# A two-layer decoder trunk on one Trainium2 core: first steps, up-panel products and delta-rule groups put in another order, and sums of squares on ScalarE

## The chip, the cores and the metric

The kernel runs on one core of a Trainium2 chip. The metric is the device time of one execution in microseconds. Five engines matter: PE (TensorE: matmuls and transposes; its weight loads are listed apart as PEld), DVE (VectorE), ACT (ScalarE), POOL (GpSimd), and SP, which issues the DMAs. Each engine takes its own instructions strictly in the order in which the program issues them, and they meet only through semaphores.

## The reference

The input is 256 tokens by 2048 features. Layer 0 mixes tokens with latent attention, layer 1 with a chunked gated delta rule; each also attends to 256 memory tokens, and each is followed by a squared-ReLU MLP. The parts that the change touches:

```python
mem_kv = mem @ mem_w_kv[i]
qkv = silu(causal_depthwise_conv(h[..., :3 * MIX_WIDTH], conv_w))      # 4 taps
q = l2_normalize(q); k = l2_normalize(k)    # x * rsqrt(sum(x * x, -1) + 1e-6), by head
kb = k * beta
L = where(strict, einsum(kb, k) * decay, 0)
u, w = triangular_solve(L + I, [v * beta, kb * exp(gc)])
a_qk = where(tril, einsum(q, k) * decay, 0)
# for each chunk of 64 tokens:
v_new = u - w @ state; o = q_dec @ state + a_qk @ v_new
state = state * g_last + k_dec.T @ v_new
o = rms_norm(o, o_norm) * silu(z)
x = layer_norm(ALPHA * x + y)
ff = square(relu(x @ mlp_w1[i])) @ mlp_w2[i]
```

## The kernel before, in words

**Weights.** They are read from HBM in chunks of 256 rows by 512 columns (512 KB), 8 chunks a panel. SP loads chunk c into one of four `raw` buffers once chunk c-4 has been split. ACT copies it to `whi` (L1031), rounded to fp32r; DVE takes the rest into `wlo` (L1394). Activations are split alike, and a product is whi by hi, whi by lo and wlo by hi, all on PE. `feed(n)` on ACT and on DVE stands for the next n splits in that engine's order; ACT's split of c waits until PE has used chunk c-4.

**Products.** `panel_t` puts 128 weight columns into PE and moves 256 tokens past them, three matmuls per block (L534, L536, L538). `panel_r` moves 512 weight columns (L587 to L589). `panel_up`, the first half of the MLP, moves hi and lo of the tokens in one matmul of 512 columns past whi (L561, "wide" below), and 256 columns past wlo (L563, "narrow"), in the order wide, narrow, wide, narrow: 16 matmuls a chunk, 128 chunks in all, 1024 pairs from k = 0 and 1024 from k = 1.

**First steps.** In 16 steps PE turns (transposes) two blocks of `mem`, later of `x`, and multiplies one chunk of the memory's key panel (steps 0 to 7, `panel_t`) or value panel (8 to 15, `panel_r`). Step k issues turn k+1 and then chunk k. DVE copies turn k+1 out (`first_out`, L1411), then takes the low part of turn k (`first_low`, L1427), then splits chunk k+1; ACT makes the high part between them (`first_hi`, L1052).

**Delta-rule groups.** Twelve heads run as three groups g of four. A group has panels q, k, v and z; q, k and v each go through a convolution (ACT scales one tap, L1279; DVE adds three, L1777; ACT takes tanh, L1283; DVE finishes, L1784), are turned into rows by PE (`conv_turns`, L852) and copied out by ACT (`rows_out`, L1290). DVE sums the squares of q and k rows (`row_sums`: a product L1805 and a reduction L1812 for each), POOL takes the power (L1993), DVE scales k and q (L1805). In `gdn` PE turns k, kb and q (L886, L891, L894), builds the decays (L899, L902), turns the decayed q (L908), forms the two score products (L912, L916), inverts the triangular matrix in six levels (L925 for level 0; L929, L939 and L942 for the others, with POOL masking the next level's block, L2093), and walks four chunks of the state. The 16 chunks of panel z and of the next group's q, called b0 to b15 here, are spread between these steps by `beside(g, i, n)`, so that PE has work while others answer.

The order is written out by hand for each engine; nothing is planned at run time. PSUM has two banks for turns, two `side` banks, and two pairs for panels, and `panel_free` counts emptied panels.

## Time and profile before

| | |
|---|---|
| median of 3 runs | 2517.56 us (2516.83 to 2519.83) |
| profiled execution | 2513.61 us, its span 2511.9 us |
| PE busy | 2399.0 us, 96% |
| PE weight loads | 2087.2 us, 83% |
| DVE / ACT / POOL busy | 59% / 42% / 10% |
| DMA | 417.10 MB, mean 166 GB/s |
| up-panel wide / narrow matmuls | 2048 of each, 399 / 281 ns each |

The "busy" of a matmul overlaps that of the next one: what a matmul costs is the distance between two starts, and this is what is read below. In the span, the first steps take about 0 to 75 us, layer 0's mixer and output to 360, its MLP to 1080, the three delta-rule groups 1155 to 1665, and the rest is layer 1's output and MLP. The slices in which PE is well below full are the first, those of the attention, and those of the delta-rule groups.

### The profile page before, as it was taken

How to read it: one execution, taken by the hardware profiler on the slowest of the kernel's cores; microseconds unless marked ns; L12 is line 12 of the kernel's file. 1: busy time of each engine (PE TensorE's matmuls, PEld its weight loads, DVE VectorE, ACT ScalarE, POOL GpSimd, SP SyncE). 2: the span in 40 equal slices, each digit the busy share in tenths (PEclk: the TensorE clock that was granted, in tenths of full speed). 3: DMA queues.
4: the chain of work that ended last, by engine and by line, in shares of the span. 5: the costliest groups of instructions: out<-in, count | busy, mean ns of one | idle time of the engine just before them, and what ended most of it. 6: DMA issues, size and time to landing. Idle time of an engine off the chain costs nothing.

```text
span 2511.9 us, 35407 instructions
## 1 busy us (share of the span) xinstructions
PE 2399.0 (96%) x13577; PEld 2087.2 (83%) x13577; DVE 1472.8 (59%) x1562; ACT 1058.3 (42%) x1244; POOL 240.9 (10%) x221
## 2 busy tenths in 40 slices
PE   7999989999999999999899899989899999999997
PEld 6897778888888888889799798878788888888885
DVE  4654567546555556576747648445765565555565
ACT  3455434434444444354424324233443443443443
POOL 0051001001000001000121211210010010000000
PEclk9999999999999999999999999989999999999998
DMA  5663356565566565655414325226455655666654
GB/s 203 201 169 109 114 197 193 193 193 184 193 184 193 195 190 185 209 168 168 135 51 143 93 60 165 62 75 211 128 191 201 191 186 193 181 201 193 189 192 159
DMA packets 234624, 417.10 MB, mean 166 GB/s; under 512 B 23761, under 2 KB 42474, under 8 KB 232938
## 3 DMA queue, kind: packets, MB, share of 16 engines
q1 hardware_dynamic: 233114, 410.73, 51.3%
q10 hardware_dynamic: 1360, 4.19, 0.4%
q8 instruction: 116, 1.90, 0.3%
q14 instruction: 34, 0.28, 0.0%
HBM read 412.77 MB, written 2.10 MB: 165 GB/s over the span
## 4 chain that ended last, share of the span: by engine, by line
PE 47%; issue 39%; DVE 8%; POOL 4%; ACT 1%; DMA 1%; POOLq 0%; ACTq 0%; DVEq 0%
PE quad L561 10%; PE quad L587 6%; PE quad L588 6%; PE quad L589 6%; PE quad L563 5%; PE quad L534 3%; PE quad L536 3%; PE quad L538 3%; DVE wlo L1394 2%; DVE cv L1777 2%; POOL hl L2061 1%; PE quad L929 1%; PE quad L942 1%; PE quad L939 1%; ACT whi L1031 1%
## 5 line engine op out<-in xcount | busy, mean ns | idle before, releaser
L1394 DVE TENSOR_TENSOR wlo<-raw,whi 128x1024 fp32r<-128x1024 f32 x760 | 977.3, 1295 | 720.0 <-ACT whi L1031 717.2
L1031 ACT ACTIVATE whi<-raw 128x1024 fp32r<-128x1024 f32 x760 | 798.8, 1058 | 991.4 <-PE quad L589 520.0
L561 PE MATMUL quad<-xs,whi 128*128 128x512 f32 x2048 | 724.2, 399 | 7.8 <-DVE xs L1657 3.7
L563 PE MATMUL quad<-xs,wlo 128*128 128x256 f32 x2048 | 574.7, 281 | 0.0
L587 PE MATMUL quad<-whi,hh 128*128 128x512 f32 x1344 | 529.3, 394 | 5.2 <-DVE hl L1532 3.8
L589 PE MATMUL quad<-whi,hl 128*128 128x512 f32 x1344 | 524.0, 390 | 0.0
L588 PE MATMUL quad<-wlo,hh 128*128 128x512 f32 x1344 | 523.8, 390 | 0.0
L561 PEld LDWEIGHTS quad<-xs,whi 128*128 128x128 f32 x2048 | 386.5, 189 | 103.1 <-issue 5.5
L563 PEld LDWEIGHTS quad<-xs,wlo 128*128 128x128 f32 x2048 | 388.4, 190 | 0.1
L587 PEld LDWEIGHTS quad<-whi,hh 128*128 128x128 f32 x1344 | 252.8, 188 | 60.8 <-issue 7.2
L589 PEld LDWEIGHTS quad<-whi,hl 128*128 128x128 f32 x1344 | 252.7, 188 | 53.1
L588 PEld LDWEIGHTS quad<-wlo,hh 128*128 128x128 f32 x1344 | 252.8, 188 | 51.7
L534 PE MATMUL quad<-xs,whi 128*128 128x256 f32 x704 | 204.1, 290 | 4.2 <-DVE wlo L1394 4.0
L536 PE MATMUL quad<-xs,whi 128*128 128x256 f32 x704 | 200.5, 285 | 0.0
L538 PE MATMUL quad<-xs,wlo 128*128 128x256 f32 x704 | 200.4, 285 | 0.0
L2061 POOL TENSOR_TENSOR hl<-relu,hh 128x1024 fp32r<-128x1024 f32 x32 | 81.0, 2530 | 1198.7 <-ACT hh L1214 1198.7
L534 PEld LDWEIGHTS quad<-xs,whi 128*128 128x128 f32 x704 | 136.3, 194 | 7.6 <-DVE wlo L1394 5.5
L538 PEld LDWEIGHTS quad<-xs,wlo 128*128 128x128 f32 x704 | 136.4, 194 | 0.0
L536 PEld LDWEIGHTS quad<-xs,whi 128*128 128x128 f32 x704 | 136.3, 194 | 0.0
L1686 DVE TENSOR_TENSOR relu<-quad,low 128x1024 f32<-128x1024 f32 x32 | 39.2, 1225 | 50.8 <-ACT low L1210 50.8
L2093 POOL TENSOR_TENSOR qr<-nt,level 128x512 f32<-128x512 f32 x36 | 53.3, 1495 | 156.4 <-DVE nt L1843 81.0
L587 PE MATMUL quad<-whi,xs 128*128 128x512 f32 x160 | 64.6, 404 | 0.0
(285 smaller groups left out, 2092.9 us busy)
## 6 DMA issues: line engine op xcount, KB each, us to landing
raw<-in_mlp_w SPq DMA_DIRECT2D x512, 512.0 KB
raw<-in_gdn_w_in SPq DMA_DIRECT2D x105, 512.0 KB
raw<-in_w_out SPq DMA_DIRECT2D x64, 512.0 KB
raw<-in_mem_w_kv SPq DMA_DIRECT2D x32, 512.0 KB
raw<-in_mla_w_in SPq DMA_DIRECT2D x25, 512.0 KB
raw<-in_mla_w_ukv SPq DMA_DIRECT2D x24, 256.0 KB
gb<-in_ln_g SPq DMA_DIRECT2D x4, 1024.0 KB, 6.6
gb<-in_ln_b SPq DMA_DIRECT2D x4, 1024.0 KB, 8.6
```

The lines of the kernel that those rows point to most:

```text
L534: nc.tensor.matmul(o, b.whi[:, slot, k, cols], ah[:, kt, :], start=start, stop=False, skip_group_check=True)
L536: nc.tensor.matmul(o, b.whi[:, slot, k, cols], al[:, kt, :], start=False, stop=False, skip_group_check=True)
L538: last = nc.tensor.matmul(o, b.wlo[:, slot, k, cols], ah[:, kt, :], start=False, stop=stop, skip_group_check=True)
L561: nc.tensor.matmul(both, b.whi[:, slot, k, cols], b.xs[:, :, kt, :], start=start, stop=False, skip_group_check=True)
L563: last = nc.tensor.matmul(ps[:, j, S:2 * S], b.wlo[:, slot, k, cols], b.xh[:, kt, :], start=False, stop=stop, skip_group_check=True)
L587: nc.tensor.matmul(ps[:, t, 0:n], ah[:, kt, toks], hi[:, k, 0:n], start=start, stop=False)
L588: nc.tensor.matmul(ps[:, t, 0:n], ah[:, kt, toks], lo[:, k, 0:n], start=False, stop=False)
L589: last = nc.tensor.matmul(ps[:, t, 0:n], al[:, kt, toks], hi[:, k, 0:n], start=False, stop=stop)
L1031: nc.scalar.activation(b.whi[:, c % NSPLIT], b.raw[:, slot], ACT.Copy).then_inc(sem.hi_ready, 1)
L1394: nc.vector.tensor_tensor(b.wlo[:, c % NSPLIT], b.raw[:, c % NRAW], b.whi[:, c % NSPLIT].bitcast(F32), ALU.subtract).then_inc(sem.lo_ready, 1)
L2061: nc.gpsimd.tensor_tensor(b.hl[:, 4 * u:4 * u + 4, :].rearrange("p k s -> p (k s)"), b.relu[:, u % 2, :], b.hh[:, 4 * u:4 * u + 4, :].rear ...
L2093: nc.gpsimd.tensor_tensor(b.bm[:, t], b.nt[:, t], b.level[:, l, :].unsqueeze(1).to_broadcast((P, GH, P)), ALU.mult).then_inc(sem.bm_set, 1)
```

## The change

It has four parts.

1. First steps: DVE takes the low part of turn k before it copies out turn k+1, and splits chunk k between the two operations of turn k; ACT makes the high part before its chunk split.
2. `panel_up`: for odd k the narrow matmul comes before the wide one (wide, narrow, narrow, wide).
3. Sums of squares of q and k rows: 16 ACT instructions of 128 elements with a running sum for each group, behind `rows_out`, in place of two products and two reductions on DVE.
4. Delta-rule groups: the turns of v go behind those of the decayed q; b2 and b3 go between the first turns; b6 goes behind level 0; ACT, DVE and their splits are put in a matching order. One split more stands before the group's last turns on both engines and one fewer after them; the gate product with z goes ahead of the wait for the output's norm.

Shortened diff (12 columns of indentation taken off):

```diff
--- before.py
+++ after.py
@@ -558,10 +558,13 @@
                     stop = ci == PANEL - 1 and k == CK - 1
-                    nc.tensor.matmul(both, b.whi[:, slot, k, cols], b.xs[:, :, kt, :], start=start, stop=False,
-                                     skip_group_check=True)
-                    last = nc.tensor.matmul(ps[:, j, S:2 * S], b.wlo[:, slot, k, cols], b.xh[:, kt, :],
-                                            start=False, stop=stop, skip_group_check=True)
+                    for half in ("hi", "lo") if k % 2 == 0 else ("lo", "hi"):
+                        if half == "hi":
+                            last = nc.tensor.matmul(both, b.whi[:, slot, k, cols], b.xs[:, :, kt, :],
+                                                    start=start, stop=stop, skip_group_check=True)
+                        else:
+                            last = nc.tensor.matmul(ps[:, j, S:2 * S], b.wlo[:, slot, k, cols], b.xh[:, kt, :],
+                                                    start=False, stop=False, skip_group_check=True)
             last.then_inc(sem.chunk_used, 1)
@@ -875,8 +878,7 @@
         tiles = range(TT)
-        beside(g, 0, 4)
-        conv_turns(g, 2)
+        beside(g, 0, 2)
         for t in tiles:
@@ -889,6 +891,7 @@
             each(lambda h, o, s_: nc.tensor.transpose(o, b.kb[:, t, h, :], b.ident[:, :]), side_ps[t], sem.p_kbt)
+        beside(g, 2)
         for t in tiles:
@@ -902,10 +905,12 @@
             last.then_inc(sem.p_gb, 1)
+        beside(g, 3)
         for t in tiles:
...
             each(lambda h, o, s_: nc.tensor.transpose(o, b.qr[:, t, h, :], b.ident[:, :]), turn_ps[t], sem.p_qdt)
+        conv_turns(g, 2)
         beside(g, 4)
@@ -915,7 +920,7 @@
                                                    skip_group_check=True), turn_ps[t], sem.p_aq)
-        beside(g, 5, 2)
+        beside(g, 5)
         for l in range(LEVELS):
@@ -929,9 +934,9 @@
                          turn_ps[t], sem.p_y)
+            beside(g, 6 + l)
             if l == 0:
                 continue
-            beside(g, 6 + l)
             for t in tiles:
@@ -1080,10 +1085,10 @@
     for k in range(2, 2 * PANEL):
-        feed(1)
+        first_hi(k)
         if k == PANEL + NSPLIT - 2:
             take_t("memk0", 0, b.km, 0, 1.0)
-        first_hi(k)
+        feed(1)
     feed(3)
@@ -1269,7 +1274,7 @@
-    def conv(g, i):
+    def conv(g, i, between=lambda: None):
         m = 3 * g + i
@@ -1279,6 +1284,7 @@
         last.then_inc(sem.conv0, 1)
+        between()
         act.wait_ge(sem.conv1, m + 1)
@@ -1290,6 +1296,15 @@
         last.then_inc(sem.panel_free, 1)
+        if i == 2:
+            return
+        act.wait_ge(sem.panel_free, PANEL_AT["qkv"[i] + str(g)] + 1)
+        for t in range(TT):
+            for h in range(GH):
+                last = nc.scalar.activation(b.th[:, h, t * P:(t + 1) * P], dst[:, t, h, :], ACT.Square,
+                                            accum_out=b.ss[:, i, t * GH + h:t * GH + h + 1])
+        if i == 1:
+            last.then_inc(sem.g_ss, 1)
@@ -1310,24 +1325,30 @@
         n0 = g * TT
-        feed(4)
-        rows_out(g, 2)
-        for t in range(TT):
-            act.wait_ge(sem.p_kt, n0 + t + 1)
-            bank_out(b.kt, t, turn_ps, sem.a_kt)
+
+        def keys_out():
+            feed(2)
+            for t in range(TT):
+                act.wait_ge(sem.p_kt, n0 + t + 1)
+                bank_out(b.kt, t, turn_ps, sem.a_kt)
+
+        conv(g, 2, keys_out)
         for t in range(TT):
...
             bank_out(b.kbt, t, side_ps, sem.a_kbt)
+        feed(1)
         for t in range(TT):
...
             nc.scalar.activation(b.dt[:, t], b.dt[:, t], ACT.Exp).then_inc(sem.a_dec, 1)
+        feed(1)
         for t in range(TT):
...
             bank_out(b.qdt, t, turn_ps, sem.a_qdt)
-        feed(3)
+        rows_out(g, 2)
+        feed(2)
         for l in range(LEVELS):
@@ -1336,8 +1357,7 @@
                 bank_out(b.ys, t, turn_ps, sem.a_y)
-            if l:
-                feed(1)
+            feed(1)
         for t in range(TT):
@@ -1349,7 +1369,7 @@
                                  ACT.Copy).then_inc(sem.a_o, 1)
-        feed(1)
+        feed(1 if g == HG - 1 else 2)
         for k in range(2):
@@ -1358,7 +1378,7 @@
         early = 3 if g else 0
-        feed(early)
+        feed(2 if g else 0)
         conv(g, 0)
@@ -1367,7 +1387,6 @@
         feed(PANEL // 2 - 1)
-        conv(g, 2)
         gdn(g)
@@ -1436,17 +1455,14 @@
-    feed(1)
-    first_out(0)
-    first_out(1)
-    first_low(0)
-    feed(1)
-    for k in range(1, 2 * PANEL):
-        if k < 2 * PANEL - 1:
-            first_out(k + 1)
+    for k in range(2 * PANEL):
+        if k < 2:
+            feed(1)
+        first_out(k)
+        if k >= 2:
+            feed(1)
         first_low(k)
-        feed(1)
-    feed(2)
+    feed(3)
     dve.wait_ge(sem.vec_t, 1)
@@ -1765,7 +1781,7 @@
-    def conv(g, i):
+    def conv(g, i, splits=0):
         m = 3 * g + i
@@ -1780,6 +1796,7 @@
         last.then_inc(sem.conv1, 1)
+        feed(splits)
         dve.wait_ge(sem.tanh1, m + 1)
@@ -1804,28 +1821,17 @@
-    def row_sums(g, i):
-
-        dve.wait_ge(sem.panel_free, PANEL_AT["qk"[i] + str(g)] + 1)
-        rows = (b.qr, b.kr)[i]
-        link(times(flat(b.dt), flat(rows), flat(rows)))
-        link(nc.vector.tensor_reduce(b.ss[:, i, :], heads(b.dt), AX.X, ALU.add))
-
     def unit_rows(g):
...
-        row_sums(g, 1)
-        nc.vector.engine_nop().then_inc(sem.g_ss, 1)
         feed(1)
...
         times(b.qr[:, :, :, :], b.qr[:, :, :, :], factor(0)).then_inc(sem.kn_set, 1)
+        times(b.kb[:, :, :, :], b.kr[:, :, :, :], per_head(b.beta, g)).then_inc(sem.kb_set, 1)
...
         n0 = g * TT
-        times(b.kb[:, :, :, :], b.kr[:, :, :, :], per_head(b.beta, g)).then_inc(sem.kb_set, 1)
-        feed(4)
-        dve.wait_ge(sem.panel_free, PANEL_AT[f"v{g}"] + 1)
-        times(b.vr[:, :, :, :], b.vr[:, :, :, :], per_head(b.beta, g))
+        feed(1)
         for t in range(TT):
@@ -1834,8 +1840,9 @@
                                     ALU.subtract).then_inc(sem.d_diff, 1)
-        times(b.kb[:, :, :, :], b.kb[:, :, :, :], per_head(b.eg, g))
-        times(b.kr[:, :, :, :], b.kr[:, :, :, :], per_head(b.ek, g)).then_inc(sem.kd_set, 1)
+        feed(1)
+        dve.wait_ge(sem.panel_free, PANEL_AT[f"v{g}"] + 1)
+        times(b.vr[:, :, :, :], b.vr[:, :, :, :], per_head(b.beta, g))
         feed(1)
@@ -1848,17 +1855,20 @@
                   b.dt[:, t].rearrange("p h c -> p (h c)")).then_inc(sem.d_aq, 1)
-        feed(2)
         eye = b.ident[:, :].unsqueeze(1).to_broadcast((P, GH, P))
-        for l in range(LEVELS):
+        for t in range(TT):
+            dve.wait_ge(sem.bm_set, g * LEVELS * TT + t + 1)
+            nc.vector.tensor_tensor(b.xt[:, t], b.bm[:, t], eye, ALU.add).then_inc(sem.d_xt, 1)
+        times(b.kb[:, :, :, :], b.kb[:, :, :, :], per_head(b.eg, g))
+        for t in range(TT):
+            dve.wait_ge(sem.a_y, g * LEVELS * TT + t + 1)
+            nc.vector.tensor_tensor(b.xi[:, t], b.ys[:, t], eye, ALU.add).then_inc(sem.d_x, 1)
+        feed(1)
+        times(b.kr[:, :, :, :], b.kr[:, :, :, :], per_head(b.ek, g)).then_inc(sem.kd_set, 1)
+        feed(1)
+        for l in range(1, LEVELS):
             for t in range(TT):
                 m = (g * LEVELS + l) * TT + t
-                if l == 0:
-                    dve.wait_ge(sem.bm_set, m + 1)
-                    nc.vector.tensor_tensor(b.xt[:, t], b.bm[:, t], eye, ALU.add).then_inc(sem.d_xt, 1)
-                    dve.wait_ge(sem.a_y, m + 1)
-                    nc.vector.tensor_tensor(b.xi[:, t], b.ys[:, t], eye, ALU.add).then_inc(sem.d_x, 1)
-                    continue
                 if l < LEVELS - 1:
@@ -1866,8 +1876,7 @@
                 nc.vector.tensor_tensor(x_, side_ps[t][:, :], x_, ALU.add).then_inc(sem.d_xt, 1)
-            if l:
-                feed(1)
+            feed(1)
         for t in range(TT):
@@ -1903,10 +1912,12 @@
         nc.vector.tensor_reduce(b.ss[:, 2, :], heads(b.nt), AX.X, ALU.add).then_inc(sem.o_ss, 1)
+        link(times(flat(b.orow), flat(b.orow), flat(b.zr)))
         feed(1)
         dve.wait_ge(sem.o_rs, g + 1)
-        link(times(b.orow[:, :, :, :], b.orow[:, :, :, :], factor(2)))
-        times(flat(b.orow), flat(b.orow), flat(b.zr)).then_inc(sem.or_set, 1)
+        times(b.orow[:, :, :, :], b.orow[:, :, :, :], factor(2)).then_inc(sem.or_set, 1)
+        if g < HG - 1:
+            feed(1)
         for k in range(2):
@@ -1915,16 +1926,14 @@
         early = 3 if g else 0
-        feed(early)
+        feed(2 if g else 0)
         conv(g, 0)
...
         conv(g, 1)
-        feed(3)
-        row_sums(g, 0)
-        feed(2)
+        feed(5)
         unit_rows(g)
         feed(2)
-        conv(g, 2)
+        conv(g, 2, 2)
         gdn(g)
```

## Rows read from the trace of the kernel before

**Rows 1.** What PE waited for, whole span: microseconds in total, times, longest.
```profile
PE quad L929 <- POOL qr L2093: 13.4, 6, 3.9
PE quad L534 <- DVE hl L1427: 12.3, 8, 2.0
...
PE quad L852 <- DVE cv L1784: 9.6, 5, 2.7
...
PE quad L628 <- DVE kb L1805: 5.3, 1, 5.3
PE quad L534 <- DVE wlo L1394: 4.0, 2, 2.0
...
PE quad L894 <- ACT kt L1306: 2.3, 2, 1.1
```

**Rows 2.** Timeline of a first step: start, duration, instruction, [idle before <-releaser].
```profile
14.84 0.60 PE L628 MATMUL quad<-ident,mrow 128*128 128x128 f32 x4
...
16.91 0.36 PE L534 MATMUL quad<-hh,whi 128*128 128x256 f32 x1 [1.47 <-DVE hl L1427]
...
23.67 1.06 ACT L1031 ACTIVATE whi<-raw 128x1024 fp32r<-128x1024 f32 x1 [6.84 <-DMA raw<-in_mem_w_kv]
```

**Rows 3.** Timeline of PE, unbroken products: first and last start of four stretches.
```profile
739.62 0.40 PE L561 MATMUL quad<-xs,whi 128*128 128x512 f32 x1
...
747.94 0.40 PE L561 MATMUL quad<-xs,whi 128*128 128x512 f32 x1
...
879.65 0.39 PE L588 MATMUL quad<-wlo,hh 128*128 128x512 f32 x1
...
885.77 0.39 PE L588 MATMUL quad<-wlo,hh 128*128 128x512 f32 x1
...
899.84 0.40 PE L561 MATMUL quad<-xs,whi 128*128 128x512 f32 x1
...
913.27 0.40 PE L561 MATMUL quad<-xs,whi 128*128 128x512 f32 x1
...
1145.14 0.28 PE L534 MATMUL quad<-xs,whi 128*128 128x256 f32 x1
...
1149.82 0.28 PE L534 MATMUL quad<-xs,whi 128*128 128x256 f32 x1
```

**Rows 4.** Timeline of PE, group 1: first z chunk, and the turns of v.
```profile
1380.35 0.40 PE L587 MATMUL quad<-whi,xs 128*128 128x512 f32 x1
...
1394.04 1.09 PE L852 MATMUL quad<-ident,cv 128*128 128x128 f32 x8 [2.61 <-DVE cv L1784]
```

**Rows 5.** Two stretches with level 1: PE, PEld, DVE, ACT, POOL busy, clock, DMA.
```profile
1240.00:1260.00 20.00, 15.89 (x85) 13.85 (x85) 9.54 (x11) 5.20 (x7) 8.21 (x6) 0.83 0.27 79
1420.00:1440.00 20.00, 19.52 (x149) 18.74 (x148) 8.37 (x12) 5.11 (x7) 7.60 (x6) 0.91 0.11 32
```

**Rows 6.** Timeline of ACT and DVE, group 1, from q's rows to v's convolution.
```profile
1354.48 1.06 ACT L1290 ACTIVATE qr<-quad 128x512 f32<-128x512 f32 x2
...
1357.72 1.55 ACT L1279 ACTIVATE cv<-quad,vcol 128x256 f32<-128x256 f32 x4
...
1366.60 3.49 DVE L1394 TENSOR_TENSOR wlo<-raw,whi 128x1024 fp32r<-128x1024 f32 x3
...
1381.95 1.23 DVE L1805 TENSOR_TENSOR kr<-kr,ss 128x1024 f32<-128x1024 f32 x1 [3.42 <-POOL ss L2082]
...
1386.62 5.01 DVE L1777 SCALAR_TENSOR_TENSOR cv<-quad,vcol,cv 128x253 f32<-128x253 f32 x12
```

**Rows 7.** Timeline of ACT in layer 0's attention: two exponentials with running sums.
```profile
222.65 0.47 ACT L1150 ACTIVATE prob<-quad,mx 128x256 f32<-128x256 f32 x1
...
223.11 0.47 ACT L1150 ACTIVATE prob<-quad,mx 128x256 f32<-128x256 f32 x1
```

**Rows 8.** ACT by shape, count | busy us, mean ns | idle before, releasers.
```profile
L1031 ACT ACTIVATE whi<-raw 128x1024 fp32r<-128x1024 f32 x760 | 798.8, 1058 | 991.4 <-PE quad L589 520.0 <-PE quad L563 287.9 <-PE quad L538 133.8
...
L1264 ACT ACT_TABLE_LOAD x1 | 1.3, 1283 | 0.0
```

## The prediction

> **What bounds the kernel now.** I read the page first: PE is busy nearly all the span, DVE a little over half, ACT and POOL less. So time can be won only where PE stands still, where its matmuls start further apart than they need, or where its clock is halved. The list of PE's waits shows where it stands still, with names [rows 1]. The reader is to see that two families matter: eight waits of `panel_t` for the low part of a turn (L1427), 12.3 us, all in the first steps; and the waits inside the delta-rule groups: level 1's L929 for POOL's mask, 13.4; the turns L852 for a convolution, 9.6; L534 for a split, 4.0; L894 for ACT, 2.3; and one turn at the end of group 2, 5.3. Then I read the timeline of each place for the order that makes the wait, starts in unbroken stretches for what a matmul really costs, and the windows for the clock.
>
> **First steps.** In step 1 PE turns blocks (start 14.84), then waits 1.47 us for DVE and starts the chunk at 16.91 [rows 2]. The order explains it: DVE copies out turn k+1 before it takes the low part of turn k, but PE issues turn k+1 just before chunk k, so chunk k always waits for a copy that it does not need. Seven steps (k = 1 to 7) pay 1.47, 10.3 us; the eighth wait of the 12.3 is the first chunk of all, which keeps its chain. From step 8 on the turns are of x and no product waits for them. In the new order copy, split and low part of turn k+1 run under chunk k: 0.6 + 1.1 + 0.6 plus hand-overs, about 2.6 us, under a chunk of 24 x 0.120 = 2.9 us [rows 3]. That just fits. What is late next is the DMA: chunk 4's split on ACT starts at 23.67 after 6.84 us of waiting for its load [rows 2]. In the new order PE would want chunk 4 at about 26.1; split (1.06), then DVE's split and low part (1.8) give 26.6. I charge 0.6. Sum: **-9.7**, bounds -7 (two more such waits) and -10.3.
>
> **Up-panel products.** The `panel_r` stretch has 27 intervals in 6.12 us, 0.2267 per wide matmul; the `panel_t` stretch 39 in 4.68, 0.1200 per narrow one [rows 3]. A wide and a narrow together should cost 0.3467. In the stretch at 739 the 24 pairs take 8.32 us, 0.3467: nothing to win. In the stretch at 899 the 38 pairs take 13.43, 0.3534: 6.7 ns too much [rows 3]. If the excess sits in the change from one length to the other, the new order has half as many changes. The mean of both stretches is 3.4 ns for 2048 pairs, 6.9 us; half is **-3.5**. Bounds: 0 (it sits in the two-part read of the wide matmul, which stays) and -13.7 (all pairs have it and all goes).
>
> **Sums of squares.** Per group, 16 instructions of 128 elements go to ACT. The nearest row is an exponential of 256 elements with a running sum: from start to start 0.46 us [rows 7], the upper bound; taking off 128 elements at L1031's 1058/1024 = 1.03 ns each [rows 8] gives 0.33, the value I take, so 8 cost 2.6 us. DVE loses two products and two reductions of about 1.2 us per group, but was waiting for POOL afterwards anyway: 3.42 us before L1805 at 1381.95 [rows 6].
> What queues behind q's eight: ACT's next split and k's first tap (L1279). Before, q's rows started at 1354.48 and took 1.06, the split filled the gap and L1279 began at 1357.72 [rows 6]. Now: 1355.5 + 0.1 + 2.6 + 0.97 for the split = 1359.2, or 1.4 late. The split that DVE does right after k's convolution (L1394 at 1366.60, done 1367.8) is that of v's fifth chunk, which PE reaches at about that moment. So a new wait of 1.2 us (1.4 less some slack) per group opens there: **+3.6** in all.
> k's eight end at about 1377.2, and DVE's product and reduction had ended at about the same time, so POOL starts no earlier; its three operations end near 1380.8 instead of 1381.9.
> A rule of the Trainium skill speaks against this part: ScalarE: Activation LUTs, Rules for kernel authors, sends multiplications to VectorE and not to ScalarE. The same page, What ACT_TABLE_LOAD costs, gives 186 ns + 0.833 ns per element with 93 ns of overlap, by which eight without the read of the sum would take 1.6 us; with that the new wait at v's fifth chunk would nearly vanish and the sum would be some 3 us better. The trace has no such instruction, so it decides nothing here.
>
> **Delta-rule groups.** From the first z chunk (1380.35) to the turns of v at 1394.04, PE does four chunks of 12 x 0.2267 = 2.7 us and then waits 2.61 for v's convolution [rows 4]. What the new order removes:
> (a) That wait in each group. L852 has five waits, 9.6 in all; the two of q's turns (0.9 each) stay, so 7.9 goes: v's turns now stand two chunks and four sets of turns later.
> (b) L929's 13.4: b6 (2.7) now lies between level 0 and level 1, and POOL's two masks (about 1.5 each, first one startable right after level 0's turns) are done by then.
> (c) L894's 2.3: b2 lies before it. Sum of (a) to (c): **-23.6**.
> (d) The clock. In the windows around level 1, group 0 shows a granted clock of 0.83 and group 1 0.91 [rows 5]: 6.8 and 3.6 us of 20 at 1.2 instead of 2.4 GHz, that is 3.4 and 1.8 us of work lost; group 2 looks like group 0. The clock fell right after the 3.9 us wait. Without that wait I give back 7.5 of the 8.6: **-7.5**.
> (e) L534's two waits of 2.02 at the start of groups 1 and 2: one split more stands before the last turns. q's convolution on DVE then starts one split (1.9) earlier and PE arrives 2.0 earlier: **-4.0** and no new wait worth a sum.
> (f) The end of group 2: the product with z leaves the chain behind POOL's power, one of two operations of 1.2: **-1.0**, and the other 4.3 of the 5.3 stays.
> (g) A new wait. ACT takes tanh of v before it copies kb's turns out, and tanh waits for v's taps on DVE: g_rs at 1380.8, three products of 1.15 (kb's is now in this chain), two splits, taps of 5.0 (L1777), tanh 1.0, first copy 0.55: 1393.4. PE, after b0, b1, two sets of turns, b2 and q's turns, wants it at 1381.5 + 8.1 + 2.6 = 1392.2. So 1.3 us per group: **+3.9**. If ACT's eight cost 0.46, it is 1 us more here and 1 at v's fifth chunk, +6 in all; if they cost less, half goes.
> The moved products with beta, eg and ek have cover: `kd_set` is wanted only after level 5. ACT's splits of b4 to b9 wait for PE's use of b0 to b5, which stand before the turns that ACT waits for next, so no cycle and no long hold.
>
> **The sum.** -9.7 - 3.5 + 3.6 - 23.6 - 7.5 - 4.0 - 1.0 + 3.9 = -41.8. The profiled execution took 2513.6 (span 2511.9), so it would take 2471.8; the median of the runs is 4.0 above it, and I predict 2517.6 - 41.8 = **2475.8**.
>
> **The rivals.**
> Forecast, its own range 2463 to 2488: chance 0.63.
> (R1) The chain of v takes the place of the waits: squares, POOL, three products, taps and tanh are slower than summed, and PE waits 3 to 5 us per group at kb's copy, with the clock falling again as in [rows 5]. For it: the chain has seven hand-overs; against it: PE now has b2 and b3 in reserve. Price 3 x (3 + 2) = 15: 2491. Chance 0.16.
> (R2) The squares need another table. ACT shows loads of 1283 ns only where a new function comes, none in the groups for copy, tanh and exp [rows 8]. If squares are not in the set that holds tanh, each set of eight brings two loads: 4 x 1.28 per group, half of it on the two chains above, so 3 x 5 = 15 us: 2491. The Trainium skill (ScalarE: Activation LUTs, Table sets: the hidden batching unit) says that cheap functions are in every set but does not name the square. Chance 0.05.
> (R3) All pairs of the up-panels have the excess and lose it, and the clock is fully kept: -10 and -2 more, 2464. Chance 0.08.
> (R4, the other side) Two matmuls of one length in a row in `panel_up` write the same bank, the second onto the columns of the first. If PE held the second weight load until the first is done, each of 1024 such places would cost the load of 0.19 beyond the 0.12 between starts, 0.07 x 1024 = 72: 2548. It is slower than before from 41 ns a place on. Against it: `panel_t` does just that, three in a row, at 0.120 [rows 3]. Chance 0.04.
> (R5) The waits only move: DMA or DVE splits bind PE as soon as it is faster and nothing is left but some us. DMA is used under a third in these windows [rows 5], which speaks against it. Time 2512 to 2518. Chance 0.04.
>
> **How the numbers follow.** A measurement of this kernel can tell about 0.2%, 5 us, from no change. Forecast, R1, R2 and R3 are faster by more: 0.92. R5 is mostly within it: 0.03. R4 and the rest of R5: 0.05. The range leaves out R4 and R5 and the far ends of R1: 2461 to 2496.
>
> **What would show it.** L1427 gone from PE's waits but for the first chunk, and perhaps one wait of about 0.6 at chunk 4; pairs of `panel_up` at (0.227 + 0.120) in all stretches; L929 and L894 without waits; a wait of about 1.3 at L899 for ACT's kbt and one of about 1 at L534 of v's fifth chunk; granted clock 1.00 around level 1. I am wrong if L899's wait is above 3 us, if table loads appear between tanh and squares, or if pairs cost over 0.36.

## The result, and the profile after

The changed kernel takes 2472.4 us in the median of four runs (2468.6 to 2472.9); the kernel before took 2517.2 in the median of its four (2514.3 to 2519.8). The ratio is 0.982, 95% interval 0.980 to 0.984: faster by 1.8%. The profiled run took 2471.89 us with a span of 2470.1, 41.8 us under the 2511.9 of before. The page of the profile after, busy time by engine and then three groups (line, engine, tiles, count, busy us, mean ns, idle time before):

```profile
span 2470.1 us, 35483 instructions
...
PE 2384.2 (97%) x13572; PEld 2078.7 (84%) x13577; DVE 1467.5 (59%) x1550; ACT 1071.8 (43%) x1340; POOL 247.9 (10%) x221
...
L563 PE MATMUL quad<-xs,whi 128*128 128x512 f32 x2048 | 649.9, 397 | 7.4 <-DVE xs L1673 3.7
...
L566 PE MATMUL quad<-xs,wlo 128*128 128x256 f32 x2048 | 403.8, 279 | 0.0
```

PE is still what bounds. The list of what PE waited for (total us, times, longest) answers to [rows 1]. L1446 is the old L1427, L855 the old L852, L902 the old L899, L934 the old L929, L631 the old L628, L1413 the old L1394:

```profile
PE quad L631 <- DVE kb L1822: 6.0, 1, 6.0
PE quad L855 <- DVE cv L1801: 5.3, 2, 2.7
...
PE quad L902 <- ACT kbt L1321: 3.6, 3, 2.0
...
PE quad L534 <- DVE hl L1446: 3.2, 2, 2.1
...
PE quad L934 <- DVE kt L1865: 1.7, 3, 0.6
...
PE quad L534 <- DVE wlo L1413: 1.5, 2, 1.1
```

Of the 12.3 us of first-step waits 3.2 are left, of level 1's 13.4 there are 1.7, the 2.3 of L894 is gone, and v's turns wait no more (of L855's waits only the two of q's turns are left). The new wait for ACT's kbt is there (L902). Where the time went, by comparing the ends of the same chunks in both traces: first steps -10.6; the stretch up to layer 0's MLP +0.9; its up-panels -3.9; the delta-rule stage -26.4; layer 1's MLP -1.7. That makes -41.7 of the 41.8. The 14.8 us less of half-clock time in the trace (83.6 before, 68.8 after, at 1.2 instead of 2.4 GHz) are 7.4 us of this. In the part with the groups (1155 to 1700 us in both traces) PE's waits fell from 43.7 to 26.0 us and the half-clock time from 44.3 to 27.2 us; 17.7 + 17.1 / 2 = 26.2, which accounts for nearly all of its 26.4.

The windows around level 1 of each group (us, then PE, PEld, DVE, ACT, POOL busy, clock, DMA share, GB/s) answer to [rows 5]: the clock is 1.00 in all three.

```profile
1225.00:1245.00 20.00, 19.45 (x134) 17.55 (x133) 18.38 (x18) 6.29 (x8) 9.71 (x6) 1.00 0.33 95
1384.00:1404.00 20.00, 19.44 (x134) 17.63 (x134) 16.86 (x16) 6.42 (x9) 12.11 (x8) 1.00 0.35 102
1541.00:1561.00 20.00, 19.44 (x135) 17.59 (x134) 17.53 (x17) 6.42 (x9) 12.77 (x8) 1.00 0.32 91
```

So the sum was right. The experiments ask whether its terms were.

### The profile page after: what moved, and what is told of

It reads as the page before. It is cut to its first block, busy times and chain, and to the rows that moved or that the text cites. A ratio compares the mean times of both kernels' runs of the same rounds, so it can differ in the third digit from the quotient of the medians.

```text
span 2470.1 us, 35483 instructions
## 1 busy us (share of the span) xinstructions
PE 2384.2 (97%) x13572; PEld 2078.7 (84%) x13577; DVE 1467.5 (59%) x1550; ACT 1071.8 (43%) x1340; POOL 247.9 (10%) x221
## 4 chain that ended last, share of the span: by engine, by line
PE 48%; issue 40%; DVE 5%; POOL 4%; ACT 2%; DMA 1%; SPq 0%; POOLq 0%; ACTq 0%; DVEq 0%
PE quad L563 10%; PE quad L592 6%; PE quad L590 6%; PE quad L591 6%; PE quad L566 5%; PE quad L534 3%; PE quad L536 3%; PE quad L538 3%; DVE cv L1793 2%; POOL hl L2070 1%; ACT whi L1036 1%; PE quad L947 1%; PE quad L934 1%; DVE wlo L1413 1%; PE quad L944 1%
## 5 line engine op out<-in xcount | busy, mean ns | idle before, releaser
L1413 DVE TENSOR_TENSOR wlo<-raw,whi 128x1024 fp32r<-128x1024 f32 x760 | 979.1, 1297 | 726.1 <-ACT whi L1036 724.0
L563 PE MATMUL quad<-xs,whi 128*128 128x512 f32 x2048 | 649.9, 397 | 7.4 <-DVE xs L1673 3.7
L592 PE MATMUL quad<-whi,hl 128*128 128x512 f32 x1344 | 523.8, 390 | 0.0
L566 PE MATMUL quad<-xs,wlo 128*128 128x256 f32 x2048 | 403.8, 279 | 0.0
L563 PEld LDWEIGHTS quad<-xs,whi 128*128 128x128 f32 x2048 | 314.6, 190 | 10.0 <-DVE wlo L1413 5.5
L592 PEld LDWEIGHTS quad<-whi,hl 128*128 128x128 f32 x1344 | 252.5, 188 | 53.1
L534 PE MATMUL quad<-xs,whi 128*128 128x256 f32 x704 | 203.5, 289 | 1.5 <-DVE wlo L1413 1.5
L538 PE MATMUL quad<-xs,wlo 128*128 128x256 f32 x704 | 199.9, 284 | 0.0
L534 PEld LDWEIGHTS quad<-xs,whi 128*128 128x128 f32 x704 | 135.8, 193 | 4.3 <-DVE wlo L1413 2.1
L536 PEld LDWEIGHTS quad<-xs,whi 128*128 128x128 f32 x704 | 135.9, 193 | 0.0
```

What stands on the lines that cost most here:

```text
L534: nc.tensor.matmul(o, b.whi[:, slot, k, cols], ah[:, kt, :], start=start, stop=False, skip_group_check=True)
L536: nc.tensor.matmul(o, b.whi[:, slot, k, cols], al[:, kt, :], start=False, stop=False, skip_group_check=True)
L538: last = nc.tensor.matmul(o, b.wlo[:, slot, k, cols], ah[:, kt, :], start=False, stop=stop, skip_group_check=True)
L563: last = nc.tensor.matmul(both, b.whi[:, slot, k, cols], b.xs[:, :, kt, :], start=start, stop=stop, skip_group_check=True)
L566: last = nc.tensor.matmul(ps[:, j, S:2 * S], b.wlo[:, slot, k, cols], b.xh[:, kt, :], start=False, stop=False, skip_group_check=True)
L592: last = nc.tensor.matmul(ps[:, t, 0:n], al[:, kt, toks], hi[:, k, 0:n], start=False, stop=stop)
```

## The experiments

"Span" is that of a kernel's one profiled execution, and a difference of two spans says less than a difference of medians: half-clock stretches fall a little otherwise in each. Medians are given first. A difference in microseconds between two kernels that ran on different occasions is beset with a microsecond or two; each ratio to the kernel before has its own interval. The diffs are shortened: arguments and lines that do not matter here are left out.

### The first steps alone

```diff
-                feed(1)
+                first_hi(k)
                 if k == PANEL + NSPLIT - 2:
                     take_t("memk0", 0, b.km, 0, 1.0)
-                first_hi(k)
+                feed(1)
```

with DVE's new loop of the first steps as in the change; all else as before.

> The kernel before with only the new order of the first steps, on ScalarE and VectorE. The prediction had 9.7 us less for it; the trace of the changed kernel stands 10.6 us earlier at the end of these steps. So 2506 to 2508 us. Rival: the gain of the first steps is given back at the next wait for a load or for the normalised input: 2514 to 2517 us.

Measured: 2506.7 against 2518.3, ratio 0.996 (0.994 to 0.997). Its trace stands 10.6 us earlier than the kernel before at the end of these steps, and at the end of the trace 8.4 are left. Of what is missing, layer 1's MLP took 2.0, where its up-panels' pairs ran at another rate in some stages (next experiment), and layer 1's attention and groups 1.3, with one half-clock stretch of 3.4 us (at 1075) that the trace of the kernel before does not have; layer 0's MLP gave 0.8 back. The first steps are worth 10.6 us by the trace and 11.6 by the medians.

### The order of the up-panels' products, undone and alone

Alone, in the kernel before:

```diff
-  matmul(both, whi, xs)            # wide, 512 columns
-  matmul(ps[S:2S], wlo, xh)        # narrow, 256 columns, for each k
+  for half in ("hi", "lo") if k % 2 == 0 else ("lo", "hi"): ...
```

> The kernel before with only the new order of the up panels' products (for each output tile all wide matmuls of the chunk, then its narrow ones). Theory A (the excess sits in the change from one length to the other): 1.7 to 6.9 us less, as the prediction had it. Theory B (a wide matmul costs 233 ns whatever stands ahead of it, because its moving operand is read in two parts): no change within 0.1%, start to start after the change still 233 ns behind a wide and 115 ns behind a narrow. The whole changed kernel showed 5.6 us less over its up panels; B would have to put that down to something else.

(The edit gives wide, narrow, narrow, wide for each output tile, as in the change, and not what the bracket of that text says.)

Undone in the changed kernel:

> The changed kernel with the old order of the up panels' products. Theory A: 1.7 to 6.9 us more than the changed kernel, 2474 to 2479 us. Theory B: within 0.1% of it, 2470 to 2474 us, with a pair from start to start at 348 to 353 ns.

Measured: alone 2512.3 against 2518.1, ratio 0.998 (0.997 to 0.999); undone 2475.6, ratio 0.984 (0.983 to 0.985) against the changed kernel's 0.982. So the order is worth 3 to 6 us, as theory A has it. But the starts tell something else than A. In the kernel with the old order, PE's timeline of two stages; between the first two rows lie 98 pairs, between the last two 60:

```profile
379.74 0.39 PE L561 MATMUL quad<-xs,whi 128*128 128x512 f32 x1
...
413.72 0.39 PE L561 MATMUL quad<-xs,whi 128*128 128x512 f32 x1
...
578.61 0.40 PE L561 MATMUL quad<-xs,whi 128*128 128x512 f32 x1
...
599.81 0.40 PE L561 MATMUL quad<-xs,whi 128*128 128x512 f32 x1
```

The distances are 33.98 / 98 = 0.3467 and 21.20 / 60 = 0.3533 us a pair. With the old order an up-panel stage runs at one of these two rates from nearly its first chunk to its last. In the kernel before 3 of the 8 stages ran at the short one; here 4 of 8, and not all the same ones. In the changed kernel, two far-apart stages, 34 pairs between the two rows of each:

```profile
585.03 0.39 PE L566 MATMUL quad<-xs,wlo 128*128 128x256 f32 x2
...
596.87 0.40 PE L566 MATMUL quad<-xs,wlo 128*128 128x256 f32 x2
...
2299.77 0.62 PE L563 MATMUL quad<-xs,whi 128*128 128x512 f32 x2
...
2311.61 0.63 PE L563 MATMUL quad<-xs,whi 128*128 128x512 f32 x2
```

11.84 / 34 = 0.3482 in both, as in every stage of every kernel with this order. The new order doesn't reach 0.3467; it takes away the chance of 0.3533. The mean over all full-clock chunks went from 350.8 ns to 348.5, times 2048 is 4.8 us.

### What makes the excess: two-part read, or change of length

```diff
-                b.xs, o = at("xs", [P, 2, KT, S], F32R, o)
+                b.xs, o = at("xs", [P, KT, 2, S], F32R, o)
```

> The changed kernel with the two halves of the input side by side in memory for each tile, so that a wide matmul reads its 512 columns in one piece and not in two of 256. Theory B (two-part read): the wide matmul falls from 233 to 227 ns from start to start, 2048 of them, so 12 to 13 us less than the changed kernel, about 2460 us. Theory A (change of length): no change, 2472 us.

Measured: 2470.7, ratio 0.982 (0.980 to 0.983), and each class of start to start is what it was (233 ns from wide to wide, 234 from wide to narrow). One piece or two makes no difference; theory B falls.

```diff
                             matmul(both, whi, xs)
+                    for j in range(4):
+                        for k in range(CK):
                             matmul(ps[S:2S], wlo, xh)
```

> The changed kernel with, for each chunk, all sixteen wide matmuls first and then all sixteen narrow ones: eight times fewer changes of length than the kernel before has. Theory A: a further loss of changes is worth up to 2 us, so 2470 to 2472 us. Theory B: the same as the changed kernel within 0.1%. Either way the first wide matmuls of a chunk no longer wait for the low half of the weights, so a stall at L563 for wlo would shorten.

(A chunk has eight of each, not sixteen as that text says.) Measured: 2472.7, ratio 0.982 (0.981 to 0.984). PE's timeline of this kernel, eight of a kind to a row:

```profile
585.47 1.12 PE L568 MATMUL quad<-xs,wlo 128*128 128x256 f32 x8
586.42 2.00 PE L561 MATMUL quad<-xs,whi 128*128 128x512 f32 x8
588.26 1.12 PE L568 MATMUL quad<-xs,wlo 128*128 128x256 f32 x8
```

A chunk takes 588.26 - 585.47 = 2.79, or 0.349 a pair: more than the changed kernel's 0.348 with a quarter of its changes of length. So theory A falls as well. The excess per chunk is 0 or 53 ns in the old order (8 x 6.7), 13 in the new (8 x 1.6), 20 in this one (8 x 2.5). I have no mechanism that gives these four numbers, and leave it open. What is shown is that the old order has two rates and the other two orders one.

### What took away level 1's waits

The prediction gave the whole 13.4 us to PE's side work b6, which now lies behind level 0. First b6 alone put back:

```diff
-                beside(g, 5)
+                beside(g, 5, 2)
                 for l in range(LEVELS):
...
-                    beside(g, 6 + l)
                     if l == 0:
                         continue
+                    beside(g, 6 + l)
```

> The changed kernel with the one piece of side work that now stands behind level 0 (beside 6) put back ahead of it, as the kernel before has it. Prediction: the wait for the level's tiles comes back, 13.4 us of waits in three groups, and part of the clock with it: 2486 to 2492 us. Rival (the wait was hidden by something else of the change, as VectorE has fewer operations now): under 5 us more, 2472 to 2477 us.

Measured: 2475.0, ratio 0.983 (0.982 to 0.984), only 2.6 us above the changed kernel; the span 5.4 above. What PE waited for at the levels:

```profile
PE quad L934 <- DVE kt L1865: 6.6, 6, 1.7
```

6.6 against 1.7: b6's place is worth 4.9 us of waits and not 13.4, and the rival of that text holds. The other 6.8 of the 13.4 stay away with b6 in its old place. So I looked at what else had stood ahead of level 1. In the kernel before, DVE's and POOL's timelines of group 1:

```profile
1413.35 1.23 DVE L1394 TENSOR_TENSOR wlo<-raw,whi 128x1024 fp32r<-128x1024 f32 x1 [2.71 <-ACT whi L1031]
1416.08 1.22 DVE L1394 TENSOR_TENSOR wlo<-raw,whi 128x1024 fp32r<-128x1024 f32 x1 [1.50 <-ACT whi L1031]
1417.22 0.68 DVE L1858 TENSOR_TENSOR kbt<-qr,ident 128x512 f32<-128x512 f32 x1
...
1418.08 1.55 POOL L2093 TENSOR_TENSOR qr<-nt,level 128x512 f32<-128x512 f32 x1 [6.59 <-DVE kbt L1858]
```

Level 0's turns on PE start at 1414.73 and are done at about 1415.8, but DVE adds the identity only at 1417.22, behind two splits that themselves waited for ACT's halves, and POOL's mask, at 1418.08, was let go by that addition. POOL is named in [rows 1] because it is last; DVE's queue made it about 2 us late. In the kernel with b6 alone put back, the same mask is let go by level 0's turns:

```profile
1395.55 2.94 POOL L2102 TENSOR_TENSOR qr<-nt,level 128x512 f32<-128x512 f32 x2 [3.99 <-PE quad L930]
```

Some 2 us in each of three groups is near the 6.8. The change takes these two splits from there, too. Putting them back and nothing else:

```diff
                 eye = b.ident[:, :].unsqueeze(1).to_broadcast((P, GH, P))
+                feed(2)
                 for t in range(TT):
...
-                feed(1)
                 times(kr, kr, ek)
-                feed(1)
```

> The changed kernel with VectorE's two splits put back ahead of level 0's additions of the identity (kt and kbt), as the kernel before has them; the side work of PE stays as changed. Putting beside 6 back ahead of level 0 had cost only 5 us of waits at the levels, not the 13.4 that the kernel before shows. Theory 1: the greater part of the 13.4 was VectorE's queue; the additions stood behind two splits, and GpSimd's next mask waits for the additions. Then waits of 2 to 4 us in all three groups come back at level 1, 5 to 10 us in all, 2478 to 2484 us. Theory 2: beside 6, which now lies between level 0 and level 1, covers the splits too: under 2 us more, 2472 to 2474 us.

Measured: 2497.5, ratio 0.992 (0.991 to 0.993), 25 us above the changed kernel: more than either theory had. Its list of waits and its windows at level 1 (of groups 0 and 1):

```profile
PE quad L934 <- DVE kt L1866: 22.9, 3, 7.6
```

```profile
1230.00:1250.00 20.00, 12.37 (x68) 11.02 (x67) 10.53 (x11) 3.49 (x5) 6.30 (x4) 0.74 0.18 53
1396.00:1416.00 20.00, 12.37 (x78) 11.47 (x77) 11.62 (x12) 3.90 (x5) 6.50 (x5) 0.83 0.19 53
```

It is 7.6 us per group. The reason stands in ACT's and DVE's timelines of the same kernel:

```profile
1396.40 1.06 ACT L1036 ACTIVATE whi<-raw 128x1024 fp32r<-128x1024 f32 x1 [1.58 <-PE quad L592]
...
1397.48 1.22 DVE L1413 TENSOR_TENSOR wlo<-raw,whi 128x1024 fp32r<-128x1024 f32 x1 [2.38 <-ACT whi L1036]
1398.63 1.28 DVE L1862 TENSOR_TENSOR kbt<-qr,ident 128x512 f32<-128x512 f32 x2
1399.83 2.28 DVE L1822 TENSOR_TENSOR kb<-kb,eg 128x1024 f32<-128x1024 f32 x1
1402.04 2.35 DVE L1866 TENSOR_TENSOR kt<-qt,ident 128x512 f32<-128x512 f32 x2
```

ACT may split a chunk only when PE has used the one four before; here the second split hangs on PE's last side chunk (L592), which is b6 itself, and then DVE's product of kb with eg (2.28 us), which the change has set between the two additions, is in the way as well. The kernel before has that product elsewhere, ahead of level 0, and ACT makes that chunk's half before its copies of level 0 and not after them; it waits 13.4 in all and not 22.9. So this run does not bring the old state back: it shows what two splits cost in the new order. Both put back together:

> The changed kernel with both put back: VectorE's two splits ahead of level 0's additions, and beside 6 ahead of level 0. If these two make the whole of what went at level 1, its waits stand at 11 to 14 us again and the clock falls there: 2484 to 2492 us. If something else of the change took a part (the masks starting earlier on GpSimd), the waits stay under 9 us: 2477 to 2483 us.

Measured: 2500.5, ratio 0.993 (0.991 to 0.994), with 24.3 us of waits at L934 (three): above both ranges of that text. It is 3 us above the run with the splits alone, as b6 alone put back is 2.6 above the changed kernel. So b6's place is worth about 3 us by the medians either way, though in waits it is 4.9 us with the splits in their new place and 1.4 with them in the old one. The splits' place decides much more. The part of the trace from layer 0's MLP to layer 1's takes 762.4 us in the changed kernel, 789.4 here and 788.8 in the kernel before: with these two pieces put back nothing of that part's gain is left. This is not their share of the change, as the product with eg now stands behind them.

### The squares back on DVE

```diff
-                for t in range(TT):
-                    for h in range(GH):
-                        last = nc.scalar.activation(b.th[:, h, t * P:(t + 1) * P], dst[:, t, h, :], ACT.Square,
-                                                    accum_out=b.ss[:, i, t * GH + h:t * GH + h + 1])
+                link(times(flat(b.dt), flat(rows), flat(rows)))
+                link(nc.vector.tensor_reduce(b.ss[:, i, :], heads(b.dt), AX.X, ALU.add))
```

> The changed kernel with the squares of the q and k rows and their sums back on VectorE (a product and a reduction for each), all else in the new order. Theory 1 (the new order of the groups carries the gain, the squares' engine matters little): ScalarE is free earlier for kb's copies and for v's taps, so the waits at L902 (2.0, 0.8, 0.8 us) and at L534 for v's fifth chunk (0.35, 1.1) shrink or go, but VectorE has about 2.2 us more before each of k's and q's rows are ready; together 0 to 4 us less to 6 us more, 2468 to 2478 us. Theory 2 (the move of the squares to ScalarE is what lets the waits for q's rows go): 8 to 24 us more, with waits at the turns of q's rows or at the panel of v back.

Measured: 2479.2, ratio 0.985 (0.983 to 0.986), 6.8 us above the changed kernel: just above the top of theory 1's range and under theory 2's, and of its mechanism. No wait is back at q's turns or at a panel; v's fifth chunk waits no more (its 1.5 us are gone); but the wait for kbt has grown:

```profile
PE quad L902 <- ACT kbt L1312: 9.6, 3, 3.4
```

ACT's, DVE's and POOL's timelines of this kernel, group 1, from ACT's copy of k's rows to POOL's first operation:

```profile
1354.42 1.07 ACT L1296 ACTIVATE kr<-quad 128x512 f32<-128x512 f32 x2
...
1356.86 1.22 DVE L1813 TENSOR_TENSOR dt<-kr 128x1024 f32<-128x1024 f32 x1
1358.11 1.22 DVE L1820 TENSOR_REDUCE ss<-dt 128x8 f32<-128x1024 f32 x1
1359.37 1.22 DVE L1404 TENSOR_TENSOR wlo<-raw,whi 128x1024 fp32r<-128x1024 f32 x1
...
1359.47 1.19 POOL L2003 TENSOR_SCALAR ss<-ss 128x16 f32<-128x16 f32 x1 [31.72 <-DVEq L1825]
```

and of the changed kernel, from ACT's copy of k's rows on:

```profile
1350.88 1.06 ACT L1296 ACTIVATE kr<-quad 128x512 f32<-128x512 f32 x2
1351.98 0.31 ACT L1304 ACTIVATE th<-kr 128x128 f32<-128x128 f32 x1
...
1352.29 0.29 ACT L1304 ACTIVATE th<-kr 128x128 f32<-128x128 f32 x1
...
1354.52 0.21 POOL L2001 TENSOR_SCALAR ss<-ss 128x16 f32<-128x16 f32 x1 [31.53 <-ACT th L1304]
```

In the changed kernel POOL starts 1354.52 - 1351.94 = 2.6 us after k's rows, with the squares on DVE 1359.47 - 1355.49 = 4.0 (the kernel before has 3.9). And POOL's first operation takes 1.19 instead of 0.21, where DVE's split has just begun. 1.4 + 1.0 = 2.4 is nearly what L902 pays more in this group (3.10 against 0.79). In all three groups L902 pays 6.0 more and v's fifth chunk 1.5 less; the half-clock time of the trace is 76.4 us against 68.8, 3.8 us of work. The squares on ACT are therefore a gain in this order, and not the cost of 3.6 that the prediction has. The squares alone on ACT in the kernel before, where no wait stands at L902's place, were not run.

### kb's copies ahead of v's tanh

```diff
                         bank_out(b.kt, t, turn_ps, sem.a_kt)
+                    for t in range(TT):
+                        act.wait_ge(sem.p_kbt, n0 + t + 1)
+                        bank_out(b.kbt, t, side_ps, sem.a_kbt)
                 conv(g, 2, keys_out)
-                for t in range(TT):
-                    act.wait_ge(sem.p_kbt, n0 + t + 1)
-                    bank_out(b.kbt, t, side_ps, sem.a_kbt)
```

> The changed kernel with ScalarE's copies of kb's turned tiles made before v's last taps, not after them. The waits at L902 (2.0, 0.8, 0.8 us) go, and in group 0 the half-clock span that starts right after that wait (3.4 us at 1215.4, worth 1.7 us). If nothing is late next: 3.6 + 1.7 = 5.3 us less, 2467 us. Rival: v's tanh and finish move behind the copies by the same time and v's turns or the scores wait instead: no change, 2472 us.

Measured: 2465.3, ratio 0.980 (0.978 to 0.981); 7.1 us under the changed kernel, span 7.3 under. The waits at L902 are gone, 3.6; only 0.8 stands at L912 in one group. Half-clock time is 62.3 us against 68.8, 3.2 us of work. 3.6 + 3.2 = 6.8. That sum is rough, as 1.7 of the 3.2 stand in layer 0's attention, which the edit does not touch; but the part from layer 0's MLP to layer 1's is itself 7.2 us shorter (755.2 against 762.4). The window that held the L902 wait of group 0 had a clock of 0.91 in the changed kernel; without the wait it is 1.00 (changed kernel first, then this one):

```profile
1210.00:1230.00 20.00, 18.03 (x103) 14.46 (x102) 14.97 (x20) 9.24 (x14) 1.40 (x2) 0.91 0.43 127
```

```profile
1208.00:1228.00 20.00, 19.20 (x115) 15.77 (x115) 17.57 (x24) 9.27 (x15) 2.54 (x2) 1.00 0.52 166
```

### The product with z behind the roots again

```diff
-                link(times(flat(b.orow), flat(b.orow), flat(b.zr)))
                 feed(1)
                 dve.wait_ge(sem.o_rs, g + 1)
-                times(orow, orow, factor(2)).then_inc(sem.or_set, 1)
+                link(times(orow, orow, factor(2)))
+                times(flat(b.orow), flat(b.orow), flat(b.zr)).then_inc(sem.or_set, 1)
```

> The changed kernel with the product by z back behind the wait for the rows' roots. By the trace of the changed kernel the early z product did not shorten the chain at the end of group 2 (from the end of the reduction to the last product 5.17 us against 4.55 before): GpSimd's two operations there took 1.10 and 2.63 us beside VectorE's fp32 products against 0.20 and 1.66. If that contention is the reason, the old order gives 0.6 us back at the last turns and nothing elsewhere: 2471 to 2472 us. If the early product helps and other work was late: 1 us more, 2473 us.

Measured: 2470.9, ratio 0.982 (0.980 to 0.983): no measurable difference by itself, but the place shows it. End of group 2 in the changed kernel, DVE, POOL, and PE's turns:

```profile
1619.42 1.22 DVE L1914 TENSOR_REDUCE ss<-nt 128x8 f32<-128x1024 f32 x1
1620.56 1.22 DVE L1822 TENSOR_TENSOR kb<-kb,zr 128x1024 f32<-128x1024 f32 x1
1621.81 1.22 DVE L1413 TENSOR_TENSOR wlo<-raw,whi 128x1024 fp32r<-128x1024 f32 x1
...
1620.73 1.10 POOL L2001 TENSOR_SCALAR ss<-ss 128x8 f32<-128x8 f32 x1 [15.14 <-DVE ss L1914]
1621.91 2.63 POOL L2002 TENSOR_TENSOR ss<-ss,mhalf 128x8 f32<-128x8 f32 x1
...
1625.86 1.97 PE L631 MATMUL quad<-ident,kb 128*128 128x128 f32 x8 [5.95 <-DVE kb L1822]
```

and with the old order:

```profile
1617.87 0.20 POOL L2001 TENSOR_SCALAR ss<-ss 128x8 f32<-128x8 f32 x1 [15.14 <-DVE ss L1914]
1618.15 1.66 POOL L2002 TENSOR_TENSOR ss<-ss,mhalf 128x8 f32<-128x8 f32 x1
...
1622.39 1.97 PE L631 MATMUL quad<-ident,kb 128*128 128x128 f32 x8 [5.34 <-DVE kb L1822]
```

In the changed kernel POOL's first operation ends when DVE's product does (0.20 becomes 1.10), and the second, which starts just after DVE's split, takes 2.63 in place of 1.66. That is 1.9 us on the chain, and only 1.2 was saved on it: the wait is 5.95 instead of 5.34.

### Both together

> The changed kernel with ScalarE's copies of kb's turned tiles ahead of v's tanh and the product by z behind the rows' roots. Apart they gave 7.1 us and 0.7 us by the medians. They touch different stages, so together 7.8 us less than the changed kernel: 2464.6 us. Rival: the half-clock spans fall differently and take one or two times 1.6 us: 2466 to 2468 us.

The edits are those of the last two experiments. Measured: 2466.1, ratio 0.979 (0.978 to 0.981), span 2464.3. It is as fast as kb's copies alone (0.980), not faster; its gain at the last turns (5.3 instead of 6.0) is there, but v's fifth chunk waits 2.6 in three groups, where the kernel with the copies alone had 0.5 in two and more half-clock time. My reading, which no run shows by itself: a PE at half its clock reaches a chunk later and finds it ready, so the one stands in for the other. Both kernels are ahead of the changed kernel in the median by 6 to 7 us; the 95% intervals of the ratios overlap a little (0.980 to 0.984, and 0.978 to 0.981).

## Why the prediction came out right, and which of its steps did not

- **First steps, -9.7.** Measured -10.6 in the trace, 11.6 alone. The mechanism held: one wait of L1446 in the first chunk, one at chunk 4. That one is 1.12, not 0.6. Each of the seven removed waits brought 1.7 and not 1.47: a step takes 5.02 us before (chunks at 16.91 and 21.93) and 3.32 after (18.61 and 21.93), as the list counts a wait only from the modelled end of the last turn.
- **Up-panels, -3.5.** Measured -5.6 (-3.9 and -1.7 by stage; 3 to 6 in the two experiments). The size is in the bounds, but the reason is wrong: "if the excess sits in the change from one length to the other" fell with the runs of eight, and its lower bound, the two-part read, with the contiguous layout. "Pairs at (0.227 + 0.120) in all stretches" did not come: they stand at 0.348.
- **Squares, +3.6.** Wrong in sign. The failed step is "so POOL starts no earlier". Counted from k's rows POOL starts 1.4 us earlier, and its first operation is free of DVE, 1.0 more; putting the squares back costs 6.8 us in all. The new wait at v's fifth chunk, from which the 3.6 came, is real but smaller: 0.35, 1.12 and 0. In size: a square costs 0.29 from start to start, not 0.33; eight are 2.35. There is no table load between tanh, square and exponential, so R2 did not occur. The Trainium skill (ScalarE: Activation LUTs, What ACT_TABLE_LOAD costs) was close here: by its figures a square of 128 elements is estimated at 0.20 us from start to start, the trace has 0.20 from an activation's start to the read of its sum, and 0.09 more to the next activation. Its rule that sends multiplications to VectorE (Rules for kernel authors) would have cost time here: DVE's way is 6.8 us slower.
- **Groups (a) to (c), -23.6.** The waits went: 7.9 at v's turns, 2.3 at L894, 13.4 less 1.7 at level 1, so 21.9; 1.2 at L908 went with them, which I had not counted. The reason for (b) was wrong. I followed the name POOL in [rows 1] and gave the gain to b6. The run shows that b6 is worth 5 us of waits. The other 6.8 went without it, and there the rows point at DVE's queue; how large its part is, no run shows, as putting the splits back cost more than the kernel before had paid. (a), (c) and (e) were not run by themselves: for them only the trace speaks.
- **(d) The clock, -7.5.** Over the whole trace 7.4, and 1.00 around level 1. That the two numbers are so close is luck: the part with the groups gave 8.5, and layer 0's attention, which the change does not touch, took 1.7 back (a half-clock stretch of 6.8 us where the other trace has 3.4). The three half-clock stretches there in the kernel before (17 us, 8.5 of work) are gone. In the whole delta-rule stage seven stretches with 30.6 us became four with 17.0, two of them at waits that are new or longer: 3.4 us behind L902's 1.97 in group 0, and 6.8 us at L855's 2.67 in group 2.
- **(e) -4.0.** From DVE's last copies of a group's end to q's turns of the next, the changed kernel takes 14.57 us (1314.85 to 1329.42), and the kernel before 16.53: -1.96 per group, twice, -3.9. But "no new wait worth a sum" was wrong: q's turns waited 0.9 and now wait 2.67. The two together show that DVE's chain, one split shorter, set this stretch before and after, and not PE's wait for the split. In PE's waits only 0.5 went (4.0 gone, 3.5 come); the other 3.4 of the 3.9 are the two half-clock stretches of 3.4 us that stand behind L534's waits in the kernel before, so they are in (d)'s measured figure as well. A wait of PE taken away is not a gain by itself; here the two numbers agree because one split is as long as that wait.
- **(f) -1.0.** Measured +0.6. "The product with z leaves the chain" is so, but it runs beside POOL's operations and holds them. The Trainium skill has this rule, which I didn't weigh (SBUF — State Buffer, Who interferes with whom): a VectorE operation with two inputs in SBUF and a GpSimd operation that reads SBUF block each other until the first is done. The trace agrees: 0.20 to 1.10 and 1.66 to 2.63.
- **(g) +3.9.** Measured 3.6 (1.97, 0.79, 0.84), and 3.2 more of clock by the run without it.

For the groups the terms, squares to (g), make -28.6, and 26.4 were measured. The waits among them make -21.1, and PE's waits fell by 17.7. They fell short at q's turns (3.5), at level 1 (1.7) and at the last turns (1.7), and did better at v's fifth chunk (2.1) and L908 (1.2). The clock gave 8.5 in place of 7.5. Outside the groups the first steps gave 0.9 more and the up-panels 2.1 more, and the stretch before layer 0's MLP took 0.9. The errors cancelled: that the total came out to within 0.1 us of the trace is luck, and what was right is that the named waits would go. The median came out 3.4 us under the 2475.8, because the prediction set it 4.0 us above the profiled run, as in the kernel before, and here it lies 0.5 above.

R1 did not occur: kb's copy was waited for under 2 us. R4 did not: there is no pair above 0.354. R3's size (all pairs at 0.3467) did not come.

## What to carry to other kernels

The engine that a wait names is the last link. Before moving PE's own work to cover such a wait, follow the named engine back one step: here the mask of POOL was late by two splits in DVE's queue, these waited for ACT, and ACT for PE. Where an engine works through a queue in order, a prefetching operation that can itself wait doesn't belong ahead of a short one on the critical chain: two splits there cost 25 us in the changed kernel.

A wait of PE can cost more than its length, as the clock may fall behind it: taking away three waits of 3.6 us in all brought 7.

## What the hardware did that I had not expected

- Pairs of one wide and one narrow matmul in alternation run at 0.3467 or 0.3533 us for a whole stage, without a visible reason, and other orders at 0.3482 or 0.349. In three traces of kernels with the old order 3, 4 and 3 of the 8 stages had the short one. With 6.7 ns x 256 pairs a stage, that is 1.7 us each, enough to blur experiments of this size.
- Reading the 512 columns in one piece or in two costs PE the same.
- The granted clock fell to half at short waits, and not at each of them: in the changed kernel 1.5 us behind 1.97 us (group 0, at L902) and at 2.67 (group 2, at L855), but not at the 2.67 of the same place in group 1. With the up-panels' old order the wait at L902's place in group 0 is 2.07 us, and the clock of that window is 1.00. So one wait taken from a trace does not tell what its clock costs.
- POOL's small operations take longer beside DVE's operations on two SBUF tiles, in three places: 0.20 to 1.10, 1.66 to 2.63, 0.21 to 1.19. The other way round, DVE's two additions of the identity to kt took 3.29 us beside POOL's mask in the changed kernel, and the two to kbt 1.28, nearly all of it alone, with the splits put back.
